# Seven half-size products for the layer-1 projections, K, Q, V and Z in single buffers on chip, and W_out written to DRAM as bf16

## The chip, the cores and the metric

The kernel runs on the 8 cores of one Trainium2 chip, each on one element of the batch; the cores exchange nothing. The metric is the device time of one execution on the slowest core, in microseconds (us).

## What is computed

Two layers, both `x <- LayerNorm(ALPHA * x + (mixer(x) * silu(z)) @ W_out)`, with S = D = 2048 per core. Layer 0 is the FoX mixer (16 heads of 128, forget gates), layer 1 is differential attention with 8 heads. Cut to layer 1, which the change touches most:

```python
def diff_mixer(h, w_in, lam_q, lam_k, subln_g, w_out, rel_bias, layer_idx):
    q, k, v, z = jnp.split(h @ w_in, [BRANCH, 2 * BRANCH, 3 * BRANCH], axis=-1)
    # q, k: (B, S, 8, 2, 128), two maps a head;  v: (B, S, 8, 256)
    for i in range(S // Q_BLOCK):            # 16 blocks of 128 rows, causal
        s = einsum('bqhmd,bkhmd->bhmqk', q[:, q0:kl], k[:, :kl]) * scale + bias
        p = softmax(where(mask, s, -inf))
        a = p[:, :, 0] - lam * p[:, :, 1]
        outs.append(einsum('bhqk,bkhe->bqhe', a.astype(v.dtype), v[:, :kl]))
    o = concatenate(outs, axis=1)
    o = o * rsqrt(mean(o * o, -1) + RMS_EPS) * subln_g * (1 - lambda_init)
    return (o * silu(z)) @ w_out
```

## The kernel before

Everything is bf16 in SBUF with f32 sums in PSUM. Two large buffers, A and B, of 65,536 bytes a partition each, hold transposed activations and then W_out; one more, M, is cut into small regions by offset (oW, oX, oS, oP, oT, oG). PSUM has eight banks `pb`.

**Order.** The code emits work items with a cost each into a planner. `Prog` derives waits from declared byte regions: an operation waits for every earlier one that wrote what it reads or used what it writes, and the region declared may be larger than the bytes touched. `Sched` carries a planner time `sc.t`; `sc.after(ns, fn)` emits `fn` once that time has gone by. `merge` and `merge_diff` weave two lists in proportion to their costs. Each engine then runs its own instructions strictly in emitted order, and so do the DMA queues: SP issues transposes, activations and outputs, POOL issues weights.

**Layer 0** projects its heads with `wino`: a 2x2 block product of half-size pieces is done as seven products instead of eight, with sums of weights and of x ahead (L401, VectorE) and sums of products behind (L546, L549, and the gate L539, VectorE). Products are 8 matmuls of 512 columns for Q and K (L498) or 32 of 128 columns for V and Z (L511). They write banks 0, 1 and 7, and the order of products is 1, 6, 7, 2, 5, 4, 3. Product 3 goes into the bank that 5 had.

**Epilogue 0** (`epi_block`, `epi_pair`): eight pairs of row blocks multiply the transposed gate (`gp0`, in B or M) by W_out (in A, loaded with a cast from f32 by the DMA of POOL's queue), 4 x 16 matmuls of 512 columns a block (`group`, L336), add the residual (L744), normalise, and write x1d (f32) and x1b (bf16, L796) to DRAM. `x1_tr` (L808) reads x1b back with a transposing DMA into B, column by column block.

**Layer 1** runs heads u = 0..7. `diff_qk` gives K and Q by plain products of 16 matmuls of 512 columns, `diff_vz` gives V and Z side by side, 16 matmuls of 512 columns for each of 16 row blocks, with a tanh, a gate (L914), a cast of V (L916) and the multiply by the norm's gain (L918), the last three on VectorE. K, Q, V and Z have two copies each, so the projections of head u run woven with the attention of head u-1. A block of attention is: scores (`mm_s`, L972), exp (L990 near the diagonal, L1014 away from it), row sums, a combination of both maps (`comb`, small operations L1031 to L1041, then L1043 over the whole row), a DMA transpose (L1048), the PV product (L1061, three accumulators in banks 5, 6, 7) and `diff_fin` (L1163 to L1184) into the gate. The maps live in a ring of 16,384 bytes, the transposed ones in another of 9,216.

**Epilogue 1** is as epilogue 0, with W_out in B and the gates in A, while the last head's attention drains.

The softmax here doesn't subtract the row's maximum and nothing guards it: scores larger than these inputs give would overflow.

## Time and profile before

| | us |
|---|---|
| median of 3 runs | 2792.17 |
| fastest and slowest run | 2779.47, 3180.02 |
| span of the profiled execution, slowest core | 2768.0 |
| spans of the eight cores | 2754.6 to 2768.0 |
| PE (TensorE) busy, share of the span | 2629.6, 95% |
| DVE (VectorE) busy | 1369.3, 49% |
| ACT (ScalarE) busy | 1240.4, 45% |
| POOL (GpSimd) busy | 214.4, 8% |

PE runs matmuls; PE's weight loads overlap them. A row of the waits names the engine that waited, its line, what it waited for, the sum, the number of times and the longest. A time is the device time of the whole execution, a span that of the profiled one from the first to the last instruction. The stages of the span: fox heads to about 1085 us, epilogue 0 to 1343 us, layer 1 from there, the heads' weave from 1456 us on, the last head and epilogue 1 from 2488 us.

### The profile page before, as it was taken

How to read it: one execution, taken by the hardware profiler on the slowest of the kernel's cores; microseconds unless marked ns; L12 is line 12 of the kernel's file. 1: busy time of each engine (PE TensorE's matmuls, PEld its weight loads, DVE VectorE, ACT ScalarE, POOL GpSimd, SP SyncE). 2: the span in 40 equal slices, each digit the busy share in tenths (PEclk: the TensorE clock that was granted, in tenths of full speed). 3: DMA queues.
4: the chain of work that ended last, by engine and by line, in shares of the span. 5: the costliest groups of instructions: out<-in, count | busy, mean ns of one | idle time of the engine just before them, and what ended most of it. 6: DMA issues, size and time to landing. Idle time of an engine off the chain costs nothing.

```text
span 2768.0 us, 60261 instructions; the slowest of 8 cores (2754.6 to 2768.0 us)
## 1 busy us (share of the span) xinstructions
PE 2629.6 (95%) x19886; PEld 1589.9 (57%) x20130; DVE 1369.3 (49%) x3834; ACT 1240.4 (45%) x3256; POOL 214.4 (8%) x412
## 2 busy tenths in 40 slices
PE   6799999999999998999999999999999999998998
PEld 4477777777777785444445544454545554543443
DVE  2544444444444443565423635455555455555666
ACT  0365555555555563343214443444444444533431
POOL 2000000000000000000000110111011111110110
PEclk9999999999999999999999999999999999999999
DMA  9222222223222239999814242534334344487653
GB/s 156 43 47 42 40 41 40 41 42 50 45 40 41 41 55 196 216 240 235 184 31 81 56 76 51 81 63 74 70 71 70 66 71 83 103 153 163 182 163 131
DMA packets 355728, 254.31 MB, mean 92 GB/s; under 512 B 280800, under 2 KB 298080, under 8 KB 350816
## 3 DMA queue, kind: packets, MB, share of 16 engines
q1 hardware_dynamic: 311184, 158.00, 24.3%
q0 software_dynamic: 44240, 92.44, 20.8%
q8 instruction: 168, 2.75, 0.4%
q14 instruction: 136, 1.11, 0.1%
HBM read 224.21 MB, written 58.26 MB: 102 GB/s over the span
## 4 chain that ended last, share of the span: by engine, by line
PE 84%; DMA 5%; DVE 3%; SPq 3%; issue 3%; ACT 1%; another core or an unknown queue 1%; DVEq 0%; POOL 0%; ACTq 0%; POOLq 0%
PE pb L336 42%; PE pb L511 13%; PE pb L498 13%; PE pb L655 4%; PE pb L640 4%; PE pb L1061 4%; PE pb L972 4%; DMA M<-M 2%; SPq L1210 1%; DMA x1b<-M 1%; DMA A<-xs 1%; DVE M L1043 1%; SPq L808 1%; ACT M L1014 1%
## 5 line engine op out<-in xcount | busy, mean ns | idle before, releaser
L643 ACT ACTIVATE M<-pb,M 128x256 bf16<-128x256 f32 (+1 forms) x1152 | 521.3, 461 | 408.5 <-PE pb L655 341.2
L336 PE MATMUL pb<-M,B 128*128 128x512 bf16 (+1 forms) x2122 | 526.2, 374 | 6.3 <-DVE M L916 3.7
L336 PE MATMUL pb<-B,M 128*128 128x512 bf16 x2058 | 517.5, 380 | 7.2 <-DMA B<-xs 3.8
L1014 ACT ACTIVATE M<-pb 128x512 bf16<-128x512 f32 (+3 forms) x512 | 264.6, 523 | 276.8 <-PE pb L972 249.1
L336 PEld LDWEIGHTS pb<-B,M 128*128 128x128 bf16 x2112 | 206.1, 98 | 204.4 <-issue 7.5
L655 PE MATMUL pb<-M 128*128 128x129 bf16 x2176 | 311.7, 221 | 1.8 <-DVE M L647 0.4
L640 PE MATMUL pb<-M 128*128 128x256 bf16 (+1 forms) x1152 | 307.0, 267 | 6.1 <-ACT M L643 4.6
L336 PEld LDWEIGHTS pb<-M,B 128*128 128x128 bf16 x2176 | 212.2, 98 | 174.7 <-issue 5.9
L655 PEld LDWEIGHTS pb<-M 128*128 128x128 bf16 x2176 | 206.5, 98 | 81.4 <-issue 5.4
L336 PE MATMUL pb<-B,A 128*128 128x512 bf16 x1002 | 236.2, 383 | 6.3 <-DMA B<-w1o 4.1
L511 PE MATMUL pb<-M,A 128*128 128x128 bf16 x3360 | 236.2, 219 | 0.1
L498 PE MATMUL pb<-A,M 128*128 128x512 bf16 x796 | 219.8, 383 | 15.2 <-DVE M L401 12.9
L511 PE MATMUL pb<-M,B 128*128 128x128 bf16 x3360 | 232.2, 219 | 2.2 <-DVE M L647 2.2
L1061 PE MATMUL pb<-M 128*128 128x256 bf16 x1088 | 210.8, 276 | 21.6 <-DMA M<-M 18.4
L972 PE MATMUL pb<-A 128*128 128x512 bf16 (+3 forms) x756 | 211.7, 319 | 17.5 <-ACT M L1014 9.3
L498 PE MATMUL pb<-B,M 128*128 128x512 bf16 x809 | 220.8, 379 | 1.5
L511 PEld LDWEIGHTS pb<-M,A 128*128 128x128 bf16 x3360 | 201.0, 98 | 3.6 <-issue 0.2
L511 PEld LDWEIGHTS pb<-M,B 128*128 128x128 bf16 x3360 | 199.4, 98 | 2.6 <-issue 2.3
L336 PE MATMUL pb<-A,B 128*128 128x512 bf16 x749 | 177.1, 384 | 15.1 <-DMA A<-w0o 14.0
L1061 PEld LDWEIGHTS pb<-M 128*128 128x128 bf16 x1088 | 105.7, 99 | 138.9 <-issue 27.6
L546 DVE TENSOR_TENSOR M<-pb,M 128x512 bf16<-128x512 f32 x150 | 103.5, 690 | 156.6 <-PE pb L640 124.8
L1043 DVE SCALAR_TENSOR_TENSOR M<-M 128x1152 bf16<-128x1152 bf16 (+15 forms) x128 | 173.0, 1352 | 5.6 <-DVE M L1041 0.4
(110 smaller groups left out, 2670.0 us busy)
## 6 DMA issues: line engine op xcount, KB each, us to landing
M<-w0s POOLq DMA_DIRECT2D x30, 1024.0 KB, 11.0
M<-x SPq DMA_DIRECT2D x16, 1024.0 KB, 6.2
x1d<-M SPq DMA_DIRECT2D x32, 512.0 KB, 5.2
M<-w1qk POOLq DMA_DIRECT2D x16, 1024.0 KB, 9.2
M<-w1vz POOLq DMA_DIRECT2D x8, 2048.0 KB, 17.2
M<-x1d SPq DMA_DIRECT2D x16, 1024.0 KB, 5.5
y<-M SPq DMA_DIRECT2D x32, 512.0 KB, 3.2
A<-w0o POOLq DMA_DIRECT2D x4, 2048.0 KB, 39.2
```

The costliest lines, as they stand in the source:

```text
L336: ins = e.matmul(out, lhsT=lhs(kc), rhs=rhs(kc), start=(kc == 0), stop=(kc == KC - 1))
L498: ins = e.matmul(pb[b][:, :], lhsT=w.ap[:, wo + kc * 128:wo + kc * 128 + 128], rhs=X.ap[:, xo + kc * 512:xo + kc * 512 + 512], start=(firs ...
L511: ins = e.matmul(pb[b][:, kk * 128:(kk + 1) * 128], lhsT=X.ap[:, xo + kc * 512 + kk * 128:xo + kc * 512 + kk * 128 + 128], rhs=w.ap[:, wo ...
L546: P.op("dve", lambda e: e.tensor_tensor(out=d, in0=shp(pb[b][:, :]), in1=shp(a.ap), op=ALU.add), reads=bank(b) + a.r, writes=rd)
L640: P.op("pe", lambda e: e.matmul(pb[s][:, 0:w], lhsT=F.k.ap[:, j * 128:(j + 1) * 128], rhs=F.q.ap[:, i0 * 128:i0 * 128 + w], start=True, st ...
L643: P.op("act", lambda e: e.activation(out=pt.ap[:, 0:w], in_=pb[s][:, 0:w], func=AF.Exp, bias=bs.ap[:, j * 8 + I:j * 8 + I + 1], scale=SCAL ...
L655: P.op("pe", lambda e, n=n, k=k, first=first: e.matmul(pb[b][:, k * 129:(k + 1) * 129], lhsT=pt.ap[:, n * 128:(n + 1) * 128], rhs=F.v3[:, ...
L808: P.dma("sp", "xt", lambda e: e.dma_start_transpose(out=d, in_=x1b[b * 128:(b + 1) * 128, :]), reads=[("x1b", b, b + 1)], writes=rx("B", t ...
L972: P.op("pe", lambda e: e.matmul(pb[s][:, o:o + nb * 128], lhsT=Dv.q3[:, m, i * 128:(i + 1) * 128], rhs=Dv.k3[:, m, j0 * 128:(j0 + nb) * 12 ...
L1014: P.op("act", lambda e: e.activation(out=self.p.ap[:, lo:lo + nb * 128], in_=pb[s][:, 0:nb * 128], func=AF.Exp, scale=SCALE, accum_out=st. ...
L1043: P.op("dve", lambda e: e.scalar_tensor_tensor(out=self.p.ap[:, 0:w], in0=self.p.ap[:, w:2 * w], scalar=c(15), in1=self.p.ap[:, 0:w], op0= ...
L1061: o = P.op("pe", lambda e, j=j: e.matmul(pb[b][:, 0:256], lhsT=self.t.ap[:, j * 128:(j + 1) * 128], rhs=Dv.v3[:, j, :], start=(j == 0), st ...
```

## The change

- Layer 1 projects by `unit1`: for each of K, Q, V, Z and each half p of the rows one unit of seven products with the class `Wino`, which layer 0 uses too. Weights come as four quarters per unit pair (`load_w1`) and get four sums of 1024 columns (`sum_w`) on VectorE. The sums of x for layer 1 take the first 49,152 bytes of A.
- With A taken, K and Q stand once in A, V and Z once in M. Projection banks are 0, 1, 7; PV accumulators 5 and 6. Head 0's K and Q, p=0, stay plain (`plain1`).
- The order of a head becomes: V and Z of head u with its upper blocks' attention, then K and Q of head u+1, p=1 and then p=0, with the lower blocks'. Where a buffer would be overwritten, `DT.clear` or a drain empties the attention first.
- The gate of Z is a multiply in place on VectorE (L961); the gain multiply is on POOL (L962). One constant of `comb` moves to POOL too; its row sums are one operation (L1095) for both maps.
- The maps, and their transposes, share one ring of 23,072 bytes with first fit. The transposed map takes the place of the second map.
- W_out of both layers is cast by DRAM-to-DRAM DMAs (`cast_wo`, 32 of them, during fox heads 1 to 8 and diff heads 1 to 4) and then loaded as bf16.
- In epilogue 0 `gp0[6]` moves from M to chunk 7 of B, and `gp0[7]` within M. Epilogue 1's buffers move.

```diff
+        def sum_w(w, base=0):
+            at = lambda k: ((k - base) % 7) * 1024
+            for out, a, b in ((4, 1, 0), (1, 3, 1), (5, 3, 4), (6, 2, 5)):
+                sl = lambda k: w.ap[:, at(k):at(k) + 1024]
+                rl = lambda k: w.rr(at(k), at(k) + 1024)
...
+        xp1 = [[V("B", p * 32768 + k * 8192, 8192) for k in range(4)] + [V("A", p * 24576 + k * 8192, 8192) for k in range(3)] for p in range(2)]
+        XSUMS = ((4, 2, 3, ALU.add), (5, 4, 0, ALU.subtract), (6, 1, 5, ALU.subtract), (2, 0, 2, ALU.subtract))
...
+                def done(k, b):
...
+                    elif k == 6:
+                        tt(T, T, b)
+                    elif k == 7:
+                        tt(U, T, b)
...
+                            copy(11, b)
+                    elif k == 5:
+                        add(22, U, b)
+                    elif k == 4:
+                        add(21, T, b)
+                    else:
+                        add(12, T, b)
+                return sum([product(k, b, f) for k, b, f in ((1, x, True), (6, y, True), (7, h, True), (2, x, False), (5, y, True), (4, h, False), (3, y, False))], [])
...
-        gp0 = [V("B", c * 8192, 8192) for c in (7, 6, 5, 4, 7, 6)] + [V("M", oS[1] + c * 8192, 8192) for c in range(2)]
+        gp0 = [V("B", c * 8192, 8192) for c in (7, 6, 5, 4, 7, 6, 7)] + [V("M", oS[1], 8192)]
...
+        wot = [[V("A", p4 * 16384, 16384) for p4 in range(4)],
+               [V("B", p4 * 16384, 16384) for p4 in range(4)]]
+        def cast_wo(li, n):
+            p4, c = n // 4, n % 4 * 2
+            P.dma("pool", "cw%d" % (n % 4), lambda e: e.dma_start(out=wob[li][p4, c:c + 2], in_=wo_in[li][p4, c:c + 2]), writes=[("wob%d" % li, n, n + 1)])
...
+        def load_wo(li, p4, h=None):
+            w = wot[li][p4]
+            lo, hi = (0, 8) if h is None else (4 * h, 4 * h + 4)
+            P.dma("pool", "wo%d_%d" % (p4, lo), lambda e: e.dma_start(out=runs(w.ap)[:, lo:hi, :], in_=wob[li][p4, lo:hi].rearrange("c p e -> p c e")),
...
+            if b >= 12:
+                sc.after(3500, lambda: x_late.append(b - 12))
...
-                s = u % 2
-                b = s * 24576
...
-                self.q = V("A", b, 8192)
-                self.k = V("A", b + 8192, 8192)
-                self.z = V("A", b + 16384, 8192)
-                self.v = V("M", oS[0] + s * 8192, 8192)
+                self.q = V("A", 49152, 8192)
+                self.k = V("A", 57344, 8192)
+                self.v = V("M", oS[0], 8192)
+                self.z = V("M", oS[0] + 8192, 8192)
...
+        w1 = [V("M", o_, WSL) for o_ in oW1]
...
+        def load_w1(u, t):
+            w = w1[t % 2]
+            P.dma("pool", "w1s%d" % (t % 2), lambda e: e.dma_start(out=runs(w.ap[:, 3072:7168]), in_=w1s[u, t].rearrange("c p e -> p c e")), writes=w.rr(3072, 7168))
...
+            def dst(c):
+                m, st = int(c % 10 == 2), 2 * p + (c > 20)
+                made(t, p, u)
+                if t in (K_, Q_):
+                    d, lo = (Dv.k, Dv.q)[t], m * 2048 + st * 512
+                    return d.ap[:, lo:lo + 512], d.rr(lo, lo + 512)
...
+            def gate(src, rsrc, H, c):
+                if H is None:
+                    return t == Z_
+                d, rd = dst(c)
+                m = int(c % 10 == 2)
+                gn = gain.ap[:, m * 128:m * 128 + 128].unsqueeze(1).to_broadcast([128, 4, 128])
+                P.op("dve", lambda e: e.scalar_tensor_tensor(out=H.ap, in0=H.ap, scalar=1.0, in1=src, op0=ALU.add, op1=ALU.mult), reads=rsrc + H.r, writes=H.r)
+                P.op("pool", lambda e: e.tensor_tensor(out=d, in0=b4(H.ap), in1=gn, op=ALU.mult), reads=H.r + gain.r, writes=rd)
+            return W1.unit(w1[t % 2], xp1[p], t in (K_, Q_), dst, gate)
...
-                P.op("dve", lambda e: e.scalar_tensor_tensor(out=zt.ap, in0=t.ap, scalar=1.0, in1=z, op0=ALU.add, op1=ALU.mult),
-                     reads=bank(b) + t.r, writes=zt.r)
-                P.op("dve", lambda e: e.tensor_copy(out=Dv.v3[:, blk, :], in_=pb[b][:, 0:256]),
-                     reads=bank(b), writes=Dv.v.rr(blk * 256, blk * 256 + 256))
-                P.op("dve", lambda e: e.tensor_tensor(out=Dv.z3[:, blk, :], in0=zt.ap, in1=gain.ap, op=ALU.mult),
-                     reads=zt.r + gain.r, writes=Dv.z.rr(blk * 256, blk * 256 + 256))
...
-                self.p = rP.get(w * 4)
+                self.p = [rP.get(w * 2), rP.get(w * 2)]
...
-                if not rA.fits(w * 2):
-                    sc.after(500, self.comb)
-                    return
...
-                        P.op("dve", lambda e, m=m: e.reduce_sum(out=c(10 + m), in_=c(m * 5, k), axis=AX.X), reads=rc(m * 5, k), writes=rc(10 + m))
...
-                    P.op("dve", lambda e: e.tensor_tensor(out=c(12, 2).unsqueeze(2), in0=c(10, 2).unsqueeze(2), in1=s3, op=ALU.add),
...
+                    s3 = st.ap[:, 0:10].rearrange("p (m c) -> p m c", m=2)[:, :, 0:k + 1]
+                    P.op("dve", lambda e: e.reduce_sum(out=c(10, 2).unsqueeze(2), in_=s3, axis=AX.X), reads=rc(0, k + 1) + rc(5, k + 1), writes=rc(10, 2))
...
-                P.op("dve", lambda e: e.scalar_tensor_tensor(out=self.p.ap[:, 0:w], in0=self.p.ap[:, w:2 * w], scalar=c(15), in1=self.p.ap[:, 0:w],
-                                                             op0=ALU.mult, op1=ALU.add),
...
+                P.op("dve", lambda e: e.scalar_tensor_tensor(out=self.p[0].ap, in0=self.p[1].ap, scalar=c(15), in1=self.p[0].ap, op0=ALU.mult, op1=ALU.add),
+                     reads=self.p[0].r + self.p[1].r + rc(15), writes=self.p[0].r)
+                P.op("pool", lambda e: e.tensor_scalar(out=c(16), in0=c(a), scalar1=c(a), scalar2=256.0 * RMS_EPS, op0=ALU.mult, op1=ALU.mult), reads=rc(a), writes=rc(16))
+                self.t = self.p[1]
...
-                    self.acc = 5 + self.no % 3
+                    self.acc = 5 + self.no % 2
...
-                free = lambda b: cnt["acc"] < 3 and b.ready is not None and (b.i % 2 or cnt["gb"] < 2)
+                free = lambda b: (cnt["acc"] < 2 and b.ready is not None and (b.i % 2 or cnt["gb"] < 2)
+                                  and own.get((V_, 0)) == b.u and (b.i < 8 or own.get((V_, 1)) == b.u) and own.get((Z_, b.i // 8)) == b.u)
...
+        def merge_diff(F, share=1.0, tail=0.0, burst=700.0, drain=True):
+            left = sum(c for c, _ in F) - tail
+            owed = DT.owed() * share
...
-                while ct < cost and cf >= lead + (tf - lead) * ct / (cost or 1):
+                while credit > 0 and owed > 0:
                     x = DT.next()
                     if x is None:
+                        credit = min(credit, burst)
...
-                    ct += x[0]
+                    credit -= x[0]
+                    owed -= x[0]
...
+                credit += it[0] * owed / max(left, it[0], 1.0)
+                left -= it[0]
                 sc.run(it)
...
+                if 1 <= u <= 8:
+                    F.insert(len(F) // 4, call(cast_wo, 0, 2 * u - 2))
+                    F.insert(3 * len(F) // 4, call(cast_wo, 0, 2 * u - 1))
...
+        pj["banks"] = [0, 1, 7]
+        for t in (K_, Q_):
+            F = plain1(0, t)
+            for n in range(len(F), 0, -4):
+                F.insert(n, call(late_sums))
+            sc.merge(F, [])
+            sum_w(w1[t], 4)
...
+        F = unit1(0, K_, 1) + [call(load_w1, 0, V_), (0.0, lambda: sc.after(13000, lambda: sum_w(w1[0], 4)))]
+        for n, f in enumerate(sum_x(xp1[0])):
+            F.insert(2 + n * 2, (0.0, f))
         sc.merge(F, [])
...
+        def nxt(u, t):
+            load_w1(u, t)
+            sc.after(14000, lambda: sum_w(w1[t % 2], 4))
+        for u in range(ND - 1):
+            F = unit1(u, V_, 1) + [call(DT.clear, u - 1)] + unit1(u, V_, 0) + [call(nxt, u + 1, K_)]
+            F += unit1(u, Z_, 1) + unit1(u, Z_, 0) + [call(nxt, u + 1, Q_)]
+            if 1 <= u < 5:
+                for n in range(4):
+                    F.insert((2 * n + 1) * len(F) // 8, call(cast_wo, 1, 4 * u - 4 + n))
+            DT.add(u, HI)
+            merge_diff(F, 0.75)
+            diff_E(u + 1)
+            DT.add(u, LO)
+            merge_diff(unit1(u + 1, K_, 1) + unit1(u + 1, Q_, 1), 0.6)
+            F = unit1(u + 1, K_, 0) + [call(nxt, u + 1, V_)] + unit1(u + 1, Q_, 0) + [call(nxt, u + 1, Z_)]
+            merge_diff(F, tail=5000)
...
+        u = ND - 1
+        DT.clear(u - 1)
+        F = unit1(u, V_, 0) + unit1(u, Z_, 0) + [call(load_wo, 1, p4) for p4 in range(2)] + [call(load_gp, p4, 0, 14) for p4 in range(3)]
+        F += unit1(u, V_, 1) + unit1(u, Z_, 1) + [call(load_wo, 1, 2), call(load_wo, 1, 3), call(load_rows, 1)]
+        DT.add(u, range(12))
+        merge_diff(F, 0.9)
```

PE, end of epilogue 0; A is W_out, B and M hold gates (`gp0`), `dq_sp_xt` are the x1 transposes and `dq_sp_gz7_0` is the load of `gp0[7]`. Before:

```order
L336 MATMUL pb<-A,M 128x512 [waits ms_dve]
L336 MATMUL pb<-A,M 128x512 x15
L336 MATMUL pb<-A,M 128x512 [waits ms_dve]
L336 MATMUL pb<-A,M 128x512 x15
L336 MATMUL pb<-A,M 128x512 [waits dq_sp_gz7_0,ms_dve]
L336 MATMUL pb<-A,M 128x512 x15
```

After:

```order
L337 MATMUL pb<-A,B 128x512 [waits ms_dve]
L337 MATMUL pb<-A,B 128x512 x13
L337 MATMUL pb<-A,B 128x512 [waits dq_sp_xt]
L337 MATMUL pb<-A,B 128x512
L337 MATMUL pb<-A,M 128x512 [waits dq_sp_gz7_0,ms_dve]
L337 MATMUL pb<-A,M 128x512 x15
```

The last two matmuls of block 13, ahead of blocks 14 and 15, now stand behind a transpose of x1.

PE, start of layer 1, where the last strip of x1 is first needed (`dq_sp_xt`). Before, after three plain strips of K and Q:

```order
L336 MATMUL pb<-B,M 128x512 [waits ms_act]
L336 MATMUL pb<-B,M 128x512 x15
L336 MATMUL pb<-B,M 128x512 [waits dq_sp_xt,ms_dve]
L336 MATMUL pb<-B,M 128x512 x15
L336 MATMUL pb<-B,M 128x512 [waits ms_dve]
L336 MATMUL pb<-B,M 128x512 x15
```

After, behind two plain strips:

```order
L337 MATMUL pb<-B,M 128x512 [waits ms_act]
L337 MATMUL pb<-B,M 128x512 x15
L514 MATMUL pb<-B,M 128x512 [waits ms_dve]
L514 MATMUL pb<-B,M 128x512 x7
L514 MATMUL pb<-A,M 128x512 [waits ms_act]
L514 MATMUL pb<-A,M 128x512 x7
```

Products of 8 matmuls, which read sums of x from A, take the place of groups of 16.

DVE, in the V,Z part of a head. Before, the gate, cast and gain operations of a row block between those of attention:

```order
L1038 RECIPROCAL M<-M 128x1
L1039 SCALAR_TENSOR_TENSOR M<-M 128x1
L1041 SCALAR_TENSOR_TENSOR M<-M 128x1
L1043 SCALAR_TENSOR_TENSOR M<-M 128x1280
L914 SCALAR_TENSOR_TENSOR M<-M,pb 128x256
L916 CAST M<-pb 128x256
L918 TENSOR_TENSOR A<-M 128x256
```

After, with L559 a product sum, L1067 the near maps, L1254 the PV output and L1102 the comb:

```order
L961 SCALAR_TENSOR_TENSOR M<-M 128x512
L559 TENSOR_TENSOR M<-pb,M 128x512
L1067 SCALAR_TENSOR_TENSOR M<-M 128x256 x2
L1254 SCALAR_TENSOR_TENSOR M<-pb,M 128x256
L559 TENSOR_TENSOR M<-pb,M 128x512
L961 SCALAR_TENSOR_TENSOR M<-M,pb 128x512
L1095 TENSOR_REDUCE M<-M 128x2
L1099 RECIPROCAL M<-M 128x1
L1100 SCALAR_TENSOR_TENSOR M<-M 128x1
L1102 SCALAR_TENSOR_TENSOR M<-M 128x1536
```

Sums of 512 columns now stand between the near maps and the combs, in the one order of DVE.

## Rows read from the trace of the kernel before

**Rows 1.** Cores: span and mean granted clock of TensorE

```profile
core 0: 2768.0 us, clock 0.987
```

**Rows 2.** First part of the page: busy time, share and instructions by engine

```profile
PE 2629.6 (95%) x19886; PEld 1589.9 (57%) x20130; DVE 1369.3 (49%) x3834; ACT 1240.4 (45%) x3256; POOL 214.4 (8%) x412
```

**Rows 3.** Windows: length, busy (x) PE, PEld, DVE, ACT, POOL, clock, DMA share, GB/s

```profile
97.00:1010.00 913.00, 905.33 (x10701) 707.16 (x10771) 428.52 (x1048) 532.63 (x1158) 20.76 (x28) 1.00 0.24 41
1070.00:1210.00 140.00, 121.66 (x723) 63.02 (x732) 64.52 (x161) 48.38 (x121) 7.01 (x14) 0.95 0.96 222
...
1455.70:1595.40 139.70, 138.91 (x727) 72.09 (x741) 72.22 (x240) 64.19 (x198) 16.11 (x31) 1.00 0.38 69
1595.40:1753.70 158.30, 146.29 (x737) 73.13 (x750) 75.23 (x247) 64.13 (x203) 17.95 (x35) 0.98 0.34 62
...
2184.60:2329.90 145.30, 141.95 (x733) 72.66 (x746) 73.89 (x244) 64.23 (x202) 17.76 (x35) 0.99 0.39 69
...
2487.70:2768.00 280.30, 250.19 (x1189) 118.18 (x1211) 175.46 (x443) 87.43 (x271) 27.57 (x54) 0.96 0.60 162
```

**Rows 4.** Waits of PE, 1455.7 to 2329.9 us: line, releaser, sum, times, longest

```profile
PE pb L972 <- ACT M L1014: 7.3, 14, 2.6
PE pb L972 <- ACT M L990: 4.6, 8, 0.7
```

**Rows 5.** Timeline of PE: start, us, engine, line, count, idle before

```profile
1344.29 55.41 PE L336 MATMUL pb<-B,M 128*128 128x512 bf16 x250 [0.96 <-DVE M L744]
1399.54 2.75 PE L336 MATMUL pb<-M,B 128*128 128x512 bf16 x12
```

**Rows 6.** Chain in order of time: start, us, what

```profile
1069.12 9.09 PE pb L511 x160
```

**Rows 7.** Timeline of PE, epilogue 0, the waits on W_out

```profile
1092.43 1.86 PE L336 MATMUL pb<-A,B 128*128 128x512 bf16 x4 [6.87 <-DMA A<-w0o]
...
1112.40 2.72 PE L336 MATMUL pb<-A,B 128*128 128x512 bf16 x6 [7.10 <-DMA A<-w0o]
```

**Rows 8.** Windows behind those waits

```profile
1092.40:1097.00 4.60, 4.57 (x15) 1.91 (x16) 0.78 (x3) 1.08 (x3) 0.00 (x0) 0.61 1.04 271
1112.40:1116.00 3.60, 3.38 (x10) 1.53 (x12) 0.00 (x0) 0.57 (x2) 0.00 (x0) 0.50 1.14 253
```

**Rows 9.** DMA issues: queue, count, KB each, us from issue to landing

```profile
A<-w0o POOLq DMA_DIRECT2D x4, 2048.0 KB, 39.2
...
B<-x1b SPq DMA_TRANSPOSE x16, 7.3
```

**Rows 10.** Timeline of SP's queue, the transposes of x1 blocks 12 and 15

```profile
1323.05 8.93 SPq L808 DMA_TRANSPOSE B<-x1b  x1
...
1364.32 6.92 SPq L808 DMA_TRANSPOSE B<-x1b  x1
```

**Rows 11.** Groups by form: busy, mean ns, idle before and what ended it

```profile
L336 PE MATMUL pb<-B,A 128*128 128x512 bf16 x1002 | 236.2, 383 | 6.3 <-DMA B<-w1o 4.1 <-DVE M L744 1.0
...
L546 DVE TENSOR_TENSOR M<-pb,M 128x512 bf16<-128x512 f32 x150 | 103.5, 690 | 156.6 <-PE pb L640 124.8 <-PE pb L498 21.3 <-PE pb L655 6.1
...
L401 DVE TENSOR_TENSOR M<-M 128x1024 bf16<-128x1024 bf16 x120 | 77.4, 686 | 4.0 <-DVE M L401 0.9 <-issue 0.2
...
L916 DVE CAST M<-pb 128x256 bf16<-128x256 f32 x128 | 53.4, 417 | 0.0
...
L539 DVE SCALAR_TENSOR_TENSOR M<-M 128x512 bf16<-128x512 f32 x30 | 20.7, 688 | 13.3 <-ACT M L535 13.3
...
L1043 DVE SCALAR_TENSOR_TENSOR M<-M 128x2048 bf16<-128x2048 bf16 x8 | 18.8, 2352 | 0.3
L1033 DVE TENSOR_TENSOR M<-M 128x2 f32<-128x2 f32 x112 | 18.1, 162 | 12.4 <-DVE M L1031 0.9
```

**Rows 12.** One line's instructions: duration in ns, least, median, longest

```profile
L1164 POOL TENSOR_TENSOR M<-M x128: 182/195/2192, 1489.8 to 2681.8; 128x1 f32<-128x1 f32 x128
...
L1165 POOL TENSOR_TENSOR M<-M x128: 549/551/2311, 1490.1 to 2682.2; 128x1 f32<-128x1 f32 x128
```

458 lines of the change are left out of this document (213 added, 245 removed).

## The prediction, made before the changed kernel had run

> **What bounds the kernel now.** I read the spans first: the slowest core takes 2768.0 us at a granted clock of 0.987 [rows 1]. The shortest of the three runs is 11.5 us above that span and the median 24.2 us, so I add 18 us to a span to get a time. The page's first part puts TensorE (PE) at 95% [rows 2]. The windows by stage say where the other 5% is: while the fox heads run (97 to 1010 us) PE is busy 905.3 of 913.0 us; a diff head takes 139.7 to 158.3 us and PE is busy at least 92% of each; the end of layer 1 has 30 us idle out of 280 [rows 3]. Inside the six middle heads the named waits of PE are small: 7.3 us for the last exponentials and 4.6 for the near ones, in six heads together [rows 4]. So the bound is the stream of matmuls itself, and a change pays if it makes that stream shorter without new waits.
>
> Two rows give the price of the stream. 256 matmuls of 512 columns run from 1344.29 to 1399.54, which is 0.2158 us each [rows 5]; 160 matmuls of 128 columns take 9.09 us, 0.0568 each [rows 6]. Half-size products over 128 columns cost 5% more per column than over 512 (4 x 0.0568 = 0.227), which the V,Z part has to pay.
>
> **(a) K and Q.** Before, a head has 256 matmuls of 512 columns for K and Q; seven products of 8, in 4 units, are 224. That is 32 fewer for seven heads and 16 fewer for the first (its p=0 stays plain): 240 x 0.2158 = **-51.8 us**.
>
> **(b) V and Z.** Before 256 x 0.2158 = 55.2 us a head; after 4 units x 7 x 32 = 896 x 0.0568 = 50.9. Eight heads: **-34.8 us**.
>
> **(c) W_out of layer 0 read as bf16.** PE waits 6.87 and 7.10 us for it [rows 7], and runs at a granted clock of 0.61 and 0.50 behind these waits [rows 8], near the lower of its two levels, for 8.2 us of work, of which about 3.6 us are lost. The load is 4 DMAs of 2 MB at 39.2 us each [rows 9]; the bf16 copy halves what is read. The next thing that is late there are the transposed gates, which share the same DMA window at a share of 0.96 [rows 3]. Between 6 and 18 us come back; I take **-14**. The 32 casts from DRAM to DRAM run beside fox heads and diff heads with DMA shares of 0.24 and 0.34 to 0.39 [rows 3] and cost nothing; with no cover, what waits would be W_out itself, as now.
>
> **(d) A new wait at the end of epilogue 0.** The gate of blocks 12 and 13 (gp0[6]) moves from M to chunk 7 of B. The order shows, two matmuls before the end of block 13, a wait on the transposes of x1 that was not there: the transpose of block 12 writes into the same declared region. Blocks 14 and 15 (128 matmuls, 27.6 us) end at 1343.33, 0.96 us before the first K,Q matmul at 1344.29 [rows 5], so block 13 ends at 1315.7. The transpose of block 12 is issued at 1323.05 [rows 10] and lands 7.3 us later [rows 9], at 1330.4. PE stands 1330.4 - 1315.7 = 14.7 us, with blocks 14 and 15 queued behind it, and some 2 us more of lower clock after the pause: **+17** (12 to 19). Behind it everything of x1 for blocks 14 and 15 is late by the same amount, so the next stage does not win it back.
>
> **(e) Start of layer 1.** Only the plain p=0 halves of K and Q, 128 matmuls or 27.6 us, now stand between the last block and the first matmul that needs the last strip; before, 192 (41.4 us). The last transpose is issued at 1364.32 [rows 10], lands at 1371.6, and 1344.29 + 27.6 = 1371.9: just covered. But the seven-product operands come after it: four sums of the late block on VectorE, 4 x 0.69 = 2.8 us, and the 16 sums of the first half, 11 us, fed between matmuls (688 ns each from L401's form [rows 11]). I take **+5** (2 to 12).
>
> **(f) Waits inside the heads.** A middle head takes 145.7 us on average ((2329.9 - 1455.7)/6) [rows 3], of which the shortest one, 139.7 us with PE idle for 0.8, is nearly pure stream. Without new waits heads go to about 145.7 - 6.9 - 4.3 = 134.5. VectorE (DVE) now works 72 to 75 us in a head [rows 3]. Off: 8 casts of 512 columns for K and Q at the 0.69 of such a sum, 16 x 3 operations of 256 columns for V and Z at the 0.417 of L916, and two small ones of about 0.16 (as L1033) in each of 16 blocks: -5.5 - 20.0 - 5.1. On: 40 product sums at 0.690, 8 gates at 0.688, 16 weight sums at 0.686: +27.6 + 5.5 + 11.0 [rows 11]. Sum 74 + 13.5, about 88 us, 65% of a head, and more in the V,Z part. In the fox heads the same scheme runs with DVE at 428.5 of 913 us (47%), and PE idle for under 1% [rows 3]. What is tight: product 3 goes into the bank of product 5 and waits for its DVE sum, with one product of 1.7 to 1.8 us (32 x 0.0568, 8 x 0.2158) ahead. The sum takes 0.69 us; a comb (L1043) in front of it holds DVE up to 2.35 us [rows 11], which leaves 2.35 + 0.69 - 1.75 = 1.3 us of stall. With 8 units in a head and a long comb in front of one in four, that is 2.6 us; add something for one accumulator less (two for three) and for single K, Q, V, Z buffers, whose forced drains cost where attention is not fed evenly: **+3 us a head, +21 over seven** (0 to 15 a head).
>
> **(g)** Epilogue 1 gets a bf16 W_out too; its wait for it was 4.1 us [rows 11], and two of the four loads come later than the others, so I count 0 (4 either way).
>
> **Sum:** -51.8 - 34.8 - 14 + 17 + 5 + 21 = **-57.6**; span 2768.0 - 57.6 = 2710, time 2710 + 18 = **2728 us**.
>
> **The POOL multiply.** The gain of Z moves to POOL: 8 multiplies of 512 per head. No row has one. From below the nearest row is POOL's own one-column multiply, L1164, 0.2 us; from above its worst, 2.2 us, since L1164 and L1165 stretch from medians of 0.195 and 0.551 us to 2.19 and 2.31 [rows 12]: about a comb's length, so POOL is held while DVE runs one. At 2.3 us each, 8 are 18 us of POOL a head, beside 18 us that it has [rows 3]: POOL stays under 30% and nobody but the PV fin of the next half head needs Z. I take 0 on the path.
> The Trainium skill (GPSIMD Engine Reference, section 3.1, Elementwise) gives about 2.6 cycles an element, an estimate of 1.1 us for 512; and SBUF — State Buffer, "Who interferes with whom", says that a DVE operation with two SBUF inputs contends with a GpSimd operation that reads SBUF, and that the first to start blocks the other. The trace agrees in one direction (L1165 up to 2.31 us); by that rule the multiply would also hold DVE, 8 x 1.1 = 9 us a head, 62 us in seven if all of it came to lie on the path, which gives about 2790.
>
> **The rivals.**
> - *The saving whole* (0.20): the fox heads show that DVE at 47% is no hindrance, and if 65% isn't either, f is 0; the loads give -18 and the transition +2: 2768 - 86.6 - 18 + 17 + 2 = 2682, time **2700**. Against it: every unit has the tight sum above.
> - *DVE and POOL in each other's way* (0.25): DVE at 65 to 70%, in the V,Z part more, long combs and POOL multiplies between its operations. If 6 to 8 us more than before stand in each head instead of 3, with up to 12 in some, f is 42 to 63: time **2749 to 2770**. Eight POOL multiplies that hold DVE for 1 us each, between the 0.2 and 2.3 of POOL's rows, give 8 x 7 = 56 and 2763; For it: the stretched L1165. Against: DVE idles over a third of the time. This is the case into which the Trainium skill's rule on the shared ports (SBUF — State Buffer, "Who interferes with whom") falls.
> - *Slower* (0.05): the sum of product 5 comes late in each unit by the longest comb, 2.35 us, in all 8 units of a head: 18.8 x 7 = 132 in place of 21, time **2839**. From (2792 - 2707)/7 = 12 us a head on the kernel is no faster (2707 being the time with f at 0). Against: only one comb in sixteen is that long [rows 11].
> - *The wait (d) is not there, or W_out's waits remain* (0.05): blocks 12 and 13 may drift so that the transpose is down in time: 2728 - 17 = 2711; or gates take the place of W_out as the late ones: 2728 + 14 = 2742. It moves the others rather than replaces them.
> - The forecast itself, **2712 to 2745**, has 0.45.
>
> **How the numbers follow.** 8 in 10 reach from a little below the whole saving (2690) to the contention case's upper part (2775). This kernel's measurement can tell about 2% from no change, and 2% below 2792 is 2736. Below that lie the whole saving (0.20), over half of the forecast (0.29) and the shifted case (0.04), with a little of the others: 0.55. Slower needs over 2848: 0.03. The rest is 0.42.
>
> **What would show it.** (a, b) PE's instruction count and the matmul groups' busy time fall; the span from the first to the last V,Z stage tells the head: 137 us right, 134 the whole saving, over 141 contention. (c) No waits on W_out behind 1090 us. (d) One wait of 12 to 17 us of PE for a transpose from x1b near the end of epilogue 0. (e) A wait on DVE sums of 2 to 10 us behind the plain K,Q. (f) Waits of PE on the lines of the product sums (L556, L559), of 1 to 2 us, many of them; POOL's multiply (L962) between 0.2 and 2.3 us. Wrong would be: heads of more than 146 us, or PE waits inside them on attention's exponentials or transposes in place of the sums.

## The result and the profile after

The changed kernel takes **2827.5 us** (median of 4 runs, 2824.9 to 2908.3) against 2785.8 for the kernel before beside it: a ratio of **1.0163**, 95% interval 1.0129 to 1.0198. The prediction was 2728 us, with a range of 2690 to 2775. Forecast and result differ in sign. Every ratio here leaves out the executions in which the cores of one die ran at a lower granted clock: one of the four of each kernel (2908.3 us here), and all six of y_share below, which has no ratio for that reason.

The cores and the first part of the page of the kernel after, which answer to [rows 1, 2]:

```profile
core 6: 2824.9 us, clock 0.968
...
PE 2575.8 (91%) x25010; PEld 1785.2 (63%) x25010; DVE 1524.6 (54%) x3572; ACT 1253.0 (44%) x3240; POOL 346.7 (12%) x644
```

PE's busy time fell by 54 us, and the span grew by 57: PE now stands still 249 us where it was 138. The ratio means 45 us. The span of the kernel before is 11.5 us under the shortest of its times, where in the other profiles 1.5 to 1.6 us lie between the two, so some 10 of the 57 us are of that one trace. To see where, the span is cut at three matmuls that both kernels have: the first of epilogue 0, the first of layer 1, and the first of epilogue 1. Windows of the kernel before, and of the one after (columns as in [rows 3]):

```profile
1078.48:1344.29 265.81, 239.39 (x1177) 113.66 (x1200) 140.97 (x345) 100.37 (x248) 15.29 (x32) 0.96 0.94 232
1344.29:2486.14 1141.85, 1106.79 (x5655) 560.72 (x5770) 560.04 (x1833) 470.87 (x1468) 132.00 (x261) 0.99 0.43 77
2486.14:2768.00 281.86, 251.75 (x1197) 118.92 (x1218) 176.31 (x445) 88.30 (x273) 28.45 (x55) 0.96 0.60 161
```

```profile
1084.26:1363.79 279.53, 239.00 (x1205) 113.31 (x1203) 140.20 (x343) 99.24 (x248) 15.28 (x32) 0.93 0.84 209
1363.79:2531.14 1167.35, 1052.53 (x10709) 759.78 (x10708) 733.38 (x1654) 503.85 (x1519) 250.91 (x475) 0.97 0.45 80
2531.14:2824.90 293.76, 245.99 (x1163) 114.33 (x1160) 159.20 (x366) 68.96 (x206) 32.87 (x57) 0.92 0.54 164
```

Epilogue 0 is 13.7 us longer, layer 1 is 25.5 longer, epilogue 1 is 11.9 longer; 5.8 us stand ahead of epilogue 0. These are the slowest cores. By the medians of the eight cores the four differences are 6.5 us ahead of epilogue 0, 6.9 in it, 20.4 in layer 1 and 13.5 in epilogue 1. Those ahead of epilogue 0 are no chance of the core: before, it starts at 1076 to 1082 us on the eight cores, after at 1084 to 1087, and in b_cast below, which has the same casts beside the fox heads, at 1077 to 1086. What they are wasn't tested. In layer 1 PE's busy time did shrink, by 54 us although six more blocks of the last head's attention are now done in it, but its idle time grew from 35 to 115 us.

Waits of PE in the six middle heads of the kernel after (1455 to 2328 us; line, releaser, sum, times, longest), the answer to [rows 4]:

```profile
PE pb L1038 <- ACT M L1080: 24.5, 11, 4.8
PE pb L1120 <- DVE M L1254: 24.4, 18, 3.0
PE pb L1038 <- ACT M L1056: 20.7, 18, 2.7
...
PE pb L527 <- DVE M L556: 0.2, 1, 0.2
```

L1038 are the scores, L1080 and L1056 the far and near exponentials, L1120 is PV, L1254 what empties its accumulator. The only wait on a product sum is the last row, 0.2 us. And the middle heads take as long as before, with a lower clock. Windows of the six together, and then of the rest of layer 1, each for the kernel before and for the one after:

```profile
1455.70:2329.90 874.20, 849.82 (x4381) 434.58 (x4468) 443.43 (x1458) 385.06 (x1204) 104.20 (x206) 0.99 0.38 68
1455.00:2328.00 873.00, 798.53 (x8121) 577.99 (x8119) 548.41 (x1243) 394.85 (x1194) 195.02 (x376) 0.97 0.45 79
...
2329.90:2486.14 156.24, 146.14 (x770) 75.52 (x784) 88.83 (x311) 71.95 (x234) 23.90 (x50) 0.99 0.68 129
2328.00:2531.14 203.14, 169.10 (x1858) 129.56 (x1856) 120.08 (x296) 79.88 (x247) 51.91 (x91) 0.94 0.48 88
```

PE is busy 133.1 us in a middle head where it was 141.6, and idle 12.4 where it was 4.1. Behind the six heads it is idle 34.0 us where it was 10.1; one wait for a far exponential there is 10.7 us long.

The timeline of PE in epilogue 0 of the kernel after shows the two waits there (idle before the row in brackets); none on W_out is left, the answer to [rows 7]:

```profile
1287.10 29.12 PE L337 MATMUL pb<-A,B 128*128 128x512 bf16 x126 [22.66 <-DMA B<-gtd]
...
1333.07 1.01 PE L337 MATMUL pb<-A,B 128*128 128x512 bf16 x2 [16.85 <-DMA B<-x1b]
```

The second was forecast, at 14.7; on the other seven cores it is 10.1 to 14.7 us. The first was 6.4 us before. It is 13.3 to 14.5 us on six of the eight cores and 22.7 and 24.6 on two; before, 4.9 to 7.4.

### The profile page after: what moved, and what is told of

Read it like the earlier page. It is cut to its first block, busy times and chain, and to the rows that moved or that the text cites. A ratio compares the mean times of both kernels' runs of the same rounds, so it can differ in the third digit from the quotient of the medians.

```text
span 2824.9 us, 70454 instructions; the slowest of 8 cores (2800.4 to 2824.9 us)
## 1 busy us (share of the span) xinstructions
PE 2575.8 (91%) x25010; PEld 1785.2 (63%) x25010; DVE 1524.6 (54%) x3572; ACT 1253.0 (44%) x3240; POOL 346.7 (12%) x644
## 4 chain that ended last, share of the span: by engine, by line
PE 75%; DMA 8%; DVE 6%; issue 4%; SPq 4%; ACT 1%; POOL 1%; DVEq 0%; another core or an unknown queue 0%; ACTq 0%; POOLq 0%
PE pb L514 25%; PE pb L527 23%; PE pb L337 13%; PE pb L688 4%; PE pb L673 4%; PE pb L1120 3%; PE pb L1038 3%; DMA M<-M 2%; DMA x1b<-M 2%; SPq L860 1%; SPq L1282 1%; DMA A<-xs 1%; DMA B<-wob 1%; DVE M L1102 1%; SPq L741 1%
## 5 line engine op out<-in xcount | busy, mean ns | idle before, releaser
L527 PE MATMUL pb<-M,B 128*128 128x128 bf16 x7456 | 539.1, 222 | 0.2 <-DVE M L556 0.2
L514 PE MATMUL pb<-B,M 128*128 128x512 bf16 x1800 | 478.1, 383 | 1.7 <-DVE M L559 1.3
L527 PE MATMUL pb<-M,A 128*128 128x128 bf16 x6432 | 452.2, 219 | 13.3 <-issue 8.4
L514 PE MATMUL pb<-A,M 128*128 128x512 bf16 x1560 | 415.8, 382 | 16.6 <-DVE M L399 12.9
L527 PEld LDWEIGHTS pb<-M,A 128*128 128x128 bf16 x6432 | 392.8, 98 | 33.0 <-issue 15.4
L559 DVE TENSOR_TENSOR M<-pb,M 128x512 f32<-128x512 f32 x322 | 221.9, 689 | 241.2 <-PE pb L527 116.1
L1080 ACT ACTIVATE M<-pb 128x512 bf16<-128x512 f32 (+3 forms) x512 | 264.9, 522 | 180.2 <-PE pb L1038 137.2
L1038 PE MATMUL pb<-A 128*128 128x256 bf16 (+3 forms) x768 | 217.8, 323 | 68.2 <-ACT M L1080 40.3
L337 PE MATMUL pb<-B,A 128*128 128x512 bf16 x1024 | 231.6, 383 | 21.1 <-DMA B<-wob 21.1
L1120 PE MATMUL pb<-M 128*128 128x256 bf16 x1088 | 203.2, 277 | 46.2 <-DVE M L1254 34.3
L556 DVE TENSOR_TENSOR M<-pb,M 128x512 bf16<-128x512 f32 x198 | 135.8, 689 | 201.4 <-PE pb L673 126.9
L337 PE MATMUL pb<-A,B 128*128 128x512 bf16 x896 | 205.8, 382 | 39.5 <-DMA B<-gtd 22.7
L514 PEld LDWEIGHTS pb<-A,M 128*128 128x128 bf16 x1560 | 143.5, 99 | 115.0 <-issue 23.5
L337 PEld LDWEIGHTS pb<-B,A 128*128 128x128 bf16 x1024 | 101.0, 99 | 137.2 <-issue 24.8
L1102 DVE SCALAR_TENSOR_TENSOR M<-M 128x1920 bf16<-128x1920 bf16 (+15 forms) x128 | 173.0, 1352 | 14.8 <-DVE M L1100 0.7
L1120 PEld LDWEIGHTS pb<-M 128*128 128x128 bf16 x1088 | 98.8, 99 | 116.7 <-issue 60.3
## 6 DMA issues: line engine op xcount, KB each, us to landing
wob<-w0o POOLq DMA_DIRECT2D x16, 512.0 KB, 13.8
```

The costliest lines, as they stand in the source:

```text
L337: ins = e.matmul(out, lhsT=lhs(kc), rhs=rhs(kc), start=(kc == 0), stop=(kc == KC - 1))
L514: ins = e.matmul(pb[b][:, :], lhsT=w.ap[:, wo + kc * 128:wo + kc * 128 + 128], rhs=xs.ap[:, kc * 512:kc * 512 + 512], start=(first and kc ...
L527: ins = e.matmul(pb[b][:, kk * 128:(kk + 1) * 128], lhsT=xs.ap[:, kc * 512 + kk * 128:kc * 512 + kk * 128 + 128], rhs=w.ap[:, wo + kc * 12 ...
L556: P.op("dve", lambda e: e.tensor_tensor(out=d, in0=shp(pb[b][:, :]), in1=shp(a.ap), op=ALU.add), reads=bank(b) + a.r, writes=rd)
L559: P.op("dve", lambda e: e.tensor_tensor(out=o.ap, in0=pb[b][:, :], in1=a.ap, op=ALU.add), reads=bank(b) + a.r, writes=o.r)
L1038: P.op("pe", lambda e: e.matmul(pb[s][:, o:o + nb * 128], lhsT=Dv.q3[:, m, i * 128:(i + 1) * 128], rhs=Dv.k3[:, m, j0 * 128:(j0 + nb) * 12 ...
```

## The experiments

My theory after the trace had four parts: the waits in the heads come from the map ring, from the casts beside the heads, and from the forced drains with their two accumulators; the wait (d) in epilogue 0 is a false one; the late gate is an order in SP's queue; and epilogue 1 waits for W_out by its own order. Rivals: the POOL multiply; and that W_out as bf16 gains nothing.

All ratios are to the kernel before, run beside each on the same chip. Each carries its 95% interval. The chips differ between experiments, so two kernels are compared by their ratios, and 0.001 of ratio is 2.8 us. The ratios of b_cast, y_base, x_castfox and f_dvegain rest on two executions each.

### W_out as bf16 alone

The edit adds the 32 casts and the bf16 load to the kernel before, at the places in the fox heads and diff heads where the change has them.

> The kernel before, with one part of the change: W_out of both layers cast to bf16 in DRAM by 32 DMAs and loaded from there. My theory (the gain moves on to the next thing that is late): the two waits on W_out in epilogue 0 (14.0 us) go, and the wait for the transposed gate of blocks 12 and 13 grows from 6.4 us to about 20 us, because SP issues that transpose in the same place; layer 1 starts within 5 us of 1344, and the whole is 0 to 8 us faster than before. Rival (c of the prediction): the gain stays, 14 us faster.

Measured: **0.9943** (0.9924 to 0.9963). The theory fell. Epilogue 0 takes 248.9 us against 265.8 on the slowest cores, so -16.9 against the -14 of the prediction, and -13.8 by the medians of the eight cores (262.5 and 248.7). The gate wait is 5.5 us there and 7.8 to 11.0 on the other seven cores: it grows by some 3 us, not to 20. Waits of PE in the six middle heads of b_cast:

```profile
PE pb L1066 <- DMA M<-M: 12.8, 6, 4.2
```

Those are PV waits on map transposes, 2.1 us in the kernel before. This is the worst of the eight cores: the others have 3.4 to 8.1 us, and 0.4 to 1.1 before. Layer 1 takes 1152 us for 1142 on the slowest cores; the medians are 1141.3 and 1140.4. The next run moves the casts that run beside the diff heads:

```diff
+                if 9 <= u <= 14:
+                    for n in range(3 * (u - 9), min(16, 3 * (u - 9) + 3)):
+                        F.insert((2 * (n % 3) + 1) * len(F) // 6, call(cast_wo, 1, n))
```

> As b_cast, but the 16 casts of layer 1's W_out run beside fox heads 9 to 14 and not beside diff heads 1 to 4. In b_cast layer 1 took 1152 us up to epilogue 1 against 1142 in the kernel before, with 12.8 us of PE waits on map transposes in six heads against 2.1. Theory: these 10 us are the casts in the way of the map transposes; they come back, and the whole is 22 to 28 us faster than before (ratio about 0.991). Rival: the 10 us are a shift of attention's order; layer 1 stays at 1150.

Measured: **0.9923** (0.9894 to 0.9952), about 21 us. Window of b_cast2 from the first V,Z load (1341.0 us) to epilogue 1 (2471.2):

```profile
1341.00:2471.20 1130.20, 1107.24 (x5733) 556.79 (x5732) 554.29 (x1821) 467.68 (x1464) 130.37 (x259) 0.99 0.40 76
```

Between the same two marks b_cast takes 1143.8 us (1342.6 to 2486.4) and the kernel before 1133.6. So on the slowest cores the casts beside the diff heads cost 13.6 us. By the medians of the eight cores layer 1 goes from 1141.3 to 1135.5, 5.8 us, and that is also what the timed ratios give: a step of 0.002, within the intervals. The waits on map transposes are down to 0.5 to 3.7 us. The casts do cost something there, nearer 6 us than 14.

### Two accumulators alone

```diff
-                    self.acc = 5 + self.no % 3
+                    self.acc = 5 + self.no % 2
...
-                free = lambda b: cnt["acc"] < 3 and b.ready is not None and (b.i % 2 or cnt["gb"] < 2)
+                free = lambda b: cnt["acc"] < 2 and b.ready is not None and (b.i % 2 or cnt["gb"] < 2)
```

> The kernel before, with one part of the change: two PV accumulators in place of three. My theory (short accumulators are one of three causes of the new waits inside the heads, about 4.5 us a head with the half clock behind them): PE's waits of PV on the line that empties the accumulator appear, 2 to 4 us a head, and the time rises by 20 to 40 us. Rival: the accumulators only bind when attention is drained in a lump, as the changed kernel does it; in the kernel before, where it is fed evenly, nothing changes (under 8 us).

Measured: **1.0003** (0.9992 to 1.0014). The rival holds: with attention fed evenly two accumulators do. The accumulator wait is 2.1 us in three times over the whole span. The time hides a shift, though: by the medians layer 1 is 8 us longer and epilogue 1 6 us shorter than in the kernel before.

### The false wait in epilogue 0

```diff
-                                    lambda k0, k1, t=t: t.rr(k0 * 256, k1 * 256)))
+                                    lambda k0, k1, t=t, lo=lo: sum([t.rr(k * 256 + lo, k * 256 + lo + 128) for k in range(k0, k1)], [])))
```

> The changed kernel, with the reads of the transposed gate in epilogue 0 declared by the columns that a block really reads, so that the last two matmuls of block 13 no longer wait for the transpose of x1 block 12. Theory: the wait of 16.9 us goes and 15 to 20 us of the time with it. Rival: the transposes of x1 for blocks 12 to 15 are late for another reason, and the wait moves to the start of layer 1; under 5 us faster.

Measured: **1.0094** (1.0078 to 1.0109), 19 us below the changed kernel. The wait is gone: block 13 reads other columns than the transpose of block 12 writes. The kernels whose names begin with x, y, z and f build on this one.

```diff
-                F.insert(12, (0.0, lambda: sc.after(8000, lambda: (load_gp0(6, 0, 16), load_gp0(7, 0, 16)))))
+                F.insert(2, (0.0, lambda: load_gp0(6, 0, 16)))
+                F.insert(12, (0.0, lambda: sc.after(8000, lambda: load_gp0(7, 0, 16))))
```

> As a_exact, and the transposing load of the gate of blocks 12 and 13 is emitted one x1 transpose and one residual load earlier in SP's queue. Theory (the wait of 22.7 us for that gate is SP's order, not the bandwidth): the load is issued some 14 us earlier and 10 to 16 us more come back than in a_exact. Rival: the transposing DMAs are limited by traffic, and the wait stays above 15 us.

Measured: **1.0087** (1.0067 to 1.0108), no step from a_exact. Another 10 to 16 us had been expected. The wait fell from 14.5 to 5.0 us on the slowest core, and on six of the eight it is gone; yet a new wait of 3.2 us stands in the plain K,Q of layer 1, on the line that empties their bank (L978). VectorE is late with it, since a sum of x ahead of it waits 3.4 us for a transpose of x1. SP's order did set the gate's wait, and taking it away doesn't move what comes next. It was tried again at the end, on the fastest version of then:

> z_share with the transposing load of the gate of blocks 12 and 13 emitted earlier, as in a_early. There PE's wait for it fell from 14.5 to 5.0 us, and the time didn't move. Theory: what follows (the last x1 transposes and their sums) ends by SP's queue, not by PE, so again within 4 us of z_share. Rival: 7 to 10 us faster.

Measured: **0.9855** (0.982 to 0.9889), z_share beside it 0.9838. No gain, as expected.

### POOL or VectorE for the gain multiply

```diff
-                P.op("pool", lambda e: e.tensor_tensor(out=d, in0=b4(H.ap), in1=gn, op=ALU.mult), reads=H.r + gain.r, writes=rd)
+                P.op("dve", lambda e: e.tensor_tensor(out=d, in0=b4(H.ap), in1=gn, op=ALU.mult), reads=H.r + gain.r, writes=rd)
```

> a_exact with the gain multiply of Z on VectorE again, 8 a head, in place of POOL. Rival of the prediction (the POOL multiply and VectorE block each other): each head gets 4 to 9 us shorter, 30 to 60 us in all. My theory now (POOL holds nobody up; the waits come from the map ring, the tanh in ACT's queue and the accumulators): no gain, and up to 10 us slower by 8 x 0.69 us more on VectorE in a head.

Measured: **1.0135** (1.0119 to 1.0151), 11 us slower than a_exact; layer 1 is 1174 us by the medians for 1160. The same edit on z_e1 (below), where no larger wait covers it:

> z_e1 with the gain multiply on VectorE. With the lumps gone it is the clean test of the rival on POOL. If POOL's multiply (1.27 us each, 8 a head) holds VectorE up, this is faster by up to 8 x 7 x 1 = 56 us. My theory: POOL holds nobody on the path; between 0 and 15 us slower than z_e1, ratio 0.975 to 0.980.

Measured: **0.9867** (0.9803 to 0.9932) against 0.9747 of z_e1: slower by 1.2%, 33 us, where at most 15 were expected; by the medians the spans are 23 us longer. So in neither kernel does the multiply on POOL cost the time that the rival gave it. One line's instructions in the kernel after, the multiply on POOL:

```profile
L962 POOL TENSOR_TENSOR M<-M x64: 1255/1273/1291, 1472.1 to 2537.4; 128x512 bf16<-128x512 f32 x64
```

But the rival's mechanism is real, and small. Two lines of VectorE that read both their inputs from SBUF, in a_exact and then in x_dvegain (shortest, median and longest in ns):

```profile
L1067 DVE SCALAR_TENSOR_TENSOR M<-M x256: 274/418/2178, 1407.0 to 2615.5; 128x256 bf16<-128x256 f32 x120, 128x128 bf16<-128x128 f32 x8
L1100 DVE SCALAR_TENSOR_TENSOR M<-M x128: 218/219/1272, 1412.7 to 2624.1; 128x1 f32<-128x1 f32 x128
...
L1067 DVE SCALAR_TENSOR_TENSOR M<-M x256: 277/419/427, 1397.0 to 2615.9; 128x256 bf16<-128x256 f32 x120, 128x128 bf16<-128x128 f32 x8
L1100 DVE SCALAR_TENSOR_TENSOR M<-M x128: 219/219/221, 1402.7 to 2624.5; 128x1 f32<-128x1 f32 x128
```

Without the multiply on POOL the long ones are gone. In the kernel after 36 instructions of VectorE are stretched, each of them beside a multiply on POOL, by 22.5 us in all, 2.8 us a head; product sums that read PSUM (L559) take 0.691 us with or without it. On VectorE the eight multiplies take 8 x 0.692 = 5.5 us a head, more than that.

### Three accumulators, two score banks

```diff
-            s = 2 + cnt["s"] % 3
+            s = 2 + cnt["s"] % 2
...
-                    self.acc = 5 + self.no % 2
+                    self.acc = 4 + self.no % 3
...
-                free = lambda b: (cnt["acc"] < 2 and b.ready is not None and (b.i % 2 or cnt["gb"] < 2)
+                free = lambda b: (cnt["acc"] < 3 and b.ready is not None and (b.i % 2 or cnt["gb"] < 2)
```

> a_exact with three PV accumulators (banks 4 to 6) and two score banks (2 and 3) in place of two and three. Theory: the waits of PV on the emptying of an accumulator (24 us in six heads) go, with the half clock behind the one of 3.0 us; but the scores wait for the exponentials more often, so that it ends between 15 us faster and 15 us slower. It tells which of the two banks is scarcer: if the score waits grow by less than 24 us in six heads, accumulators were.

Measured: **1.0091** (1.0075 to 1.0107), as a_exact. The accumulator waits (24.4 us in six heads) are gone, and the score waits went from 24.1 and 20.7 to 36.0 and 27.0 us. The score waits grew by 18.2 us, less than the 24.4 that went, so by the rule set ahead of the run the accumulators were the scarcer ones; but the time doesn't move. Two scarce banks change places.

### The map ring

The slot of the first map goes back to the planner 5 us after the comb is emitted. The edit makes it 9:

```diff
-                sc.after(5000 + w, lambda: rP.live.remove(self.p[0]))
+                sc.after(9000 + w, lambda: rP.live.remove(self.p[0]))
```

> a_exact with a slot of the map ring given free 4 us later in the planner's time, so that the next map isn't written where a transpose still reads. Theory: ACT's wait on a map transpose (23.3 us, 7 times in six heads) goes, PE's wait behind it (3.6 us a head, 4.6 with the near one) falls to under 1 us, and with the half clock behind it 4 to 6 us a head come back: 25 to 40 us. Rival: the ring is simply too small at that point; the planner then holds scores back and has to drain them in a lump at the end of the stage, where the waits reappear; within 10 us of a_exact.

Measured: **0.9980** (0.9969 to 0.9990), 31 us below a_exact. One thing that it does is seen on ACT. Waits of ACT in the six middle heads, in the kernel after and in x_ring (core 1):

```profile
ACT M L1080 <- DMA M<-M: 23.3, 7, 4.7
```

```profile
ACT M L1080 <- DMA M<-M: 10.8, 5, 3.4
```

An exponential may not write a slot that a transpose still reads. It stands at the head of ACT's queue until the transpose has landed, and the scores of the next blocks stand behind it, PE with them. This wait was to go and only halves, and it isn't the whole gain. PE's waits on the far exponentials in these heads fall from 24.5 to 15.3 us, those on an accumulator from 24.4 to 17.9, and those on the near exponentials rise from 20.7 to 25.9. By the medians of cores 0 to 3 against a_exact, 18 of the gained us lie in the six middle heads, 9 ahead of head 0's first gate and 5 behind the middle heads. A later release shifts the whole weave of scores and projections, and the runs don't part the wait for the transpose from that shift. Then the casts are moved as in b_cast2, once without the ring's edit and once with it:

> a_exact with only the casts of layer 1's W_out moved beside fox heads 9 to 14 (the ring's slots are given free as early as in the changed kernel). It separates the two causes that y_base takes away together. If the early release alone makes exponentials wait for a transpose that still reads, the wait of 3.6 us a head stays and the gain is under 10 us (ratio to before 1.006 or more). If it takes a transpose that the casts made late, the waits go in all heads and the ratio is as y_base's, 0.993 to 0.998.

Measured: **1.0098** (1.0074 to 1.0123); ACT still waits 20.9 us in six times. The casts alone were not the cause.

> x_ring with the casts of layer 1's W_out beside fox heads 9 to 14, not beside diff heads. Theory: casts make the map transposes land late, and a late transpose is what keeps the map ring busy, so the remaining waits of ACT on a map transpose (11.1 us in six heads in x_ring) go, and heads 1 to 4 get 1 to 2 us shorter each: 8 to 15 us faster than x_ring (ratio to before 0.998), so about 0.994. Rival: with the later release the ring no longer depends on the casts; within 4 us of x_ring.

Measured: **0.9933** (0.9911 to 0.9954), and no wait of ACT on a map transpose is left. Heads on its core 5 take 139.6 us each. So the two causes hang together. As I read it, with the early release a transpose is in the way in any case, with the later one only those that the casts make late. One head of y_base in four windows (the Z units; K,Q p=1 and K p=0; Q p=0; the V units), and under it the same four of the kernel after:

```profile
1557.41:1599.93 42.52, 38.23 (x538) 33.78 (x536) 29.69 (x57) 20.00 (x61) 17.87 (x21) 1.00 0.36 59
1599.93:1651.92 51.99, 49.04 (x263) 25.75 (x262) 34.61 (x98) 20.54 (x65) 12.61 (x28) 0.97 0.36 68
1651.92:1665.64 13.72, 13.72 (x89) 7.50 (x88) 6.09 (x11) 3.88 (x12) 4.01 (x10) 1.00 0.53 97
1665.64:1697.01 31.37, 30.54 (x471) 27.40 (x469) 21.45 (x46) 20.52 (x63) 1.59 (x6) 1.00 0.53 86
```

```profile
1601.01:1647.99 46.98, 39.16 (x528) 35.33 (x526) 27.20 (x51) 19.00 (x54) 14.97 (x20) 0.93 0.49 82
1647.99:1702.29 54.30, 50.59 (x272) 26.60 (x271) 34.73 (x99) 22.41 (x72) 11.08 (x31) 0.97 0.33 60
1702.29:1715.98 13.69, 13.69 (x89) 7.51 (x87) 6.09 (x11) 3.99 (x12) 4.04 (x10) 1.00 0.55 97
1715.98:1747.23 31.25, 30.41 (x471) 27.40 (x470) 23.26 (x49) 20.36 (x63) 2.93 (x9) 1.00 0.78 120
```

The 6.6 us between the sums lie in the first two windows. In the first the clock is 1.00 for 0.93: PE's pause of 3.6 us had cost its own length and a stretch at the lower level behind it.

> y_base with slots given free another 4 us later (13 in place of 9 us). Theory: 9 us covered most, so at most 5 us faster; if the ring is now too small, waits come back as drains and it is 5 to 20 us slower. It brackets the best time of release.

Measured: **0.9955** (0.9940 to 0.9971): slower, if anything. The accumulator waits doubled (17.8 to 34.3 us). By the medians layer 1 is 34 us longer and epilogue 1, with less attention left for it, 20 us shorter. So between 9 and 13 us the release no longer pays in the heads; values between weren't tried.

### The forced drain

```diff
-            merge_diff(unit1(u + 1, K_, 1) + unit1(u + 1, Q_, 1), 0.6)
+            merge_diff(unit1(u + 1, K_, 1) + unit1(u + 1, Q_, 1), 0.8)
```

> y_base with 0.8 in place of 0.6 of the owed attention woven into the K,Q p=1 units, so that less is left for the forced drain behind them. Theory: the wait of 3.0 us on an accumulator in each head belongs to that forced drain and goes, with the half clock behind it: 3 to 5 us a head, 20 to 35 us. Rival: attention then runs short in the units of p=0, or the drain only moves; within 8 us.

It has no ratio. In its trace, on cores 4 to 7, a head takes 136.5 us for 139.6. The same kernel again:

> y_share again, timed: in its profile the four cores of the second die show heads of 136.5 us against 139.6 in y_base, and the accumulator wait of 3.0 us a head gone. Theory: 3 us a head in seven heads, about 22 us under y_base, ratio to before 0.984 to 0.988. Rival: the next stage pays it back; 0.993.

Measured: **0.9838** (0.9815 to 0.9860), 26 us below y_base; by the medians 19 of them lie in the heads, and most of the rest ahead of epilogue 0, which y_base, on another chip, starts 7 us later. Waits of PE in the middle heads of y_base (core 7) and of z_share:

```profile
PE pb L1120 <- DVE M L1254: 17.8, 6, 3.1
```

```profile
PE pb L1120 <- DVE M L1254: 1.3, 6, 0.3
```

K of the next head overwrites the one buffer of K, so all scores of the lower blocks must be out first; what was not woven in ran in a lump. That its short PV groups used two accumulators faster than VectorE empties them is my reading; what is shown is that the wait goes when the lump gets smaller.

### The tanh ahead of the exponentials

The edit emits the tanh of Z's gate 0.9 us after the sum that it reads, in place of directly behind it. In it, a gate can read a sum that the next part has overwritten, so only its order counts.

> y_base with the tanh of Z's gate emitted 0.9 us later in the planner's time, so that ACT does not stand at it, with exponentials behind it, while VectorE still makes the sum. Theory: PE's waits on the near exponentials (25 us in six heads) fall by 10 us or more, 5 to 15 us faster than y_base. Rival: these waits are the plain length of one exponential between two score groups; nothing changes.

Measured: **0.9939** (0.9919 to 0.9958), as y_base. The near waits fell from 25.9 to 7.9 us, and the accumulator waits rose from 17.8 to 29.4. With 0.5 and 0.6 us, on z_e1:

> z_e1 with the tanh of Z's gate emitted 0.5 us later and its multiply 0.6 us after that (1.1 us in all, as long as before). In y_tanh, with 0.9 and 0.7, the waits on the near exponentials fell from 25.9 to 7.9 us in six heads, but those on an accumulator rose from 17.8 to 29.4. Theory: with the drain woven in (z_share) the accumulators have room, so the gain stays: 10 to 20 us faster than z_e1, ratio to before 0.968 to 0.971. Rival: the waits only change place again; 0.974 to 0.976.

Measured: **0.9765** (0.9716 to 0.9813) against 0.9747. The near waits are 16.8 us for 31.1 in the whole span, and the time doesn't move; why it doesn't stays open.

### Epilogue 1

```diff
+            if n == 0 and li:
+                order = [(pa, 0), (pa, 1), (pb_, 0), (pb_, 1), (pa, 2), (pb_, 2), (pa, 3), (pb_, 3)]
...
-            merge_diff(F, 1.0 / max(1, 4 - n))
+            merge_diff(F, (0.6, 0.6, 0.8)[n] if n < 3 else 1.0)
```

> z_share with epilogue 1 rearranged: its first two blocks multiply the first two quarters of W_out before either needs the third, and more of the last head's attention is woven into the first blocks. Theory: PE's wait of 17 to 21 us on the third quarter, which can be loaded only after the last projection, falls to under 8 us and 8 to 15 us come back. Rival: the queues of SP and POOL then hold up the transposes of the gate; no gain.

Measured: **0.9747** (0.9728 to 0.9766), 2702 us: 25 us below z_share and 70 below the kernel before. The two edits were not parted, and the gain is larger than the 8 to 15 us expected; all of it lies in epilogue 1 (290.5 to 262.7 us by the medians). The wait on W_out (21.7 us in z_share) does not show any more; a wait of 9.2 us for the residual addition that empties a bank (L789) is new. Its page:

```profile
PE 2554.3 (95%) x25010; PEld 1770.5 (66%) x25010; DVE 1525.2 (56%) x3572; ACT 1246.3 (46%) x3240; POOL 379.6 (14%) x644
```

This version beats both kernels. It has all of the change, and six edits of order and declaration on it.

## Why the prediction was wrong, by its own steps

- **What bounds the kernel.** Right as a reading, wrong as a rule for what comes next. PE's stream did bind; once it is shorter, waits that were small or hidden before are what binds.
- **(a), (b)** Right, and seen where the new waits are mostly gone: in five heads of z_share, at a granted clock of 1.00, PE is busy 130.1 us a head. The 141.6 of before less the 11.2 forecast are 130.4. Layer 1 was forecast at 1141.8 - 86.6 + 21 + 5 = 1081 us, 1094 with the attention moved into it (see g); z_share takes 1096 by the median.
- **(c)** -14 forecast, -13.8 by the medians in b_cast and -16.9 on the slowest cores. Right. In the changed kernel the wait for the gate of blocks 12 and 13 grew from between 4.9 and 7.4 us to between 13.3 and 24.6. "The transposed gates" were named as the next late thing and priced at nothing. The faster W_out alone doesn't do that (5.5 to 11.0 us in b_cast); the order of SP's queue does (a_early), and what makes that queue later in the changed kernel stays open. Nor does the wait have a price of its own, since without it the time stays. With (d) taken away epilogue 0 is 9.3 us shorter than before by the medians, 13.7 in z_e1. That the casts cost nothing was wrong in the diff heads, by about 6 us (b_cast2), 14 on the slowest cores.
- **(d)** Right, mechanism and size: 16.85 us for 14.7 on the slowest core, 10.1 to 14.7 on the others, and 19 us with what follows for 17. It was read from the order alone.
- **(e)** The waits there sum to 5.3 us (2.7, 2.2 and 0.4) for 5. Right. 4.9 of them are waits on product sums (L556, L559) that stand between the sums of x in VectorE's order.
- **(f)** This is the step that failed. The price was put on the sum behind product 5: 3 us a head. There PE waits 0.2 us in six heads; VectorE worked 91 us a head, close to the 88 forecast, and no product sum held PE up. The wait was in the attention: (24.5 + 24.4 + 20.7)/6 = 11.6 us a head. PE's idle time is 12.4 us a head where 4.1 + 3 were forecast, and its busy time 133.1 where the shorter stream would be 130.4, 2.7 more at a lower granted clock (0.97). So a head took 145.5 us where 137.5 was forecast, 48 us in the six middle heads. The prediction's own sign of being wrong, waits on attention's exponentials in place of the sums, is what came. "Single K, Q, V, Z buffers, whose forced drains cost" stood in the step as a thing to be added and had no number; and the one map ring, which the section on the change names, was in no step. The later release of its slots is the largest single gain, 31 us, against 26 for the smaller drain.
- **(g)** Forecast 0. Epilogue 1 is 11.9 us longer although 57 of 136 tile columns of the last head's attention have left it, some 13 us by the prices of [rows 5, 6]. So it was wrong by 25 us: the two late loads of W_out make a wait of 21.1 us. The prediction had seen them and took the wait of before, 4.1 us, as the size.
- **The POOL multiply.** 0 on the path was assumed. Each takes 1.273 us, inside the bounds of 0.2 and 2.3, and together they stretch VectorE's instructions by 2.8 us a head. What of that reaches the path isn't known; moving the multiplies to VectorE costs more.
- **The rivals.** "DVE and POOL in each other's way" names a mechanism that the trace shows, at a fraction of its price; as the cause of the slowdown it is out by two runs. The slower rival had nearly the right size (2839) and the wrong place, which is luck. Its point of decision, 12 us a head, was nearly reached by another mechanism (11 us over the 134.5 of a head without new waits). Its chance of 0.05 counted only one way in which a head can lose 12 us.
- By stage, against a span of 2710: epilogue 0 and what is ahead of it +16.5, layer 1 +86, epilogue 1 +12, together 115. Of the 86, 13 are the attention that came over from epilogue 1 and 48 stand in the six middle heads; the other 25 weren't taken apart, but PE's idle time behind these heads (34.0 us for 10.1) is where most of them must be. In times the miss is 99.5 us, 2827.5 for 2728: the trace of before has a span well under the times of that kernel, which the 18 us added to it made up for.

## What to carry to other kernels

When a change turns double buffers into single ones to pay for a shorter stream, price the lumps and not the averages: list what must be empty before each buffer is written again, and see how long the queue, the ring and the banks take for what is then done in one go. A ring whose slots are given back by a planned time is a wait of its own: compare that time with when the reader's DMA really lands. A wait of some microseconds that stands just behind the one you remove needs a price too: ask what sets it, and what stands behind it in turn. Here the gate's wait grew, and taking it away gained nothing, since the next thing was as late. And a false dependency can be seen in the order of instructions before anything has run.

## What the runs showed of the hardware that was not expected

- POOL multiplies 512 f32 elements a partition, with bf16 out, in 1.273 us, and nearly the same each time (1.255 to 1.291). Beside it VectorE gives way: instructions with both inputs in SBUF are stretched, L399 (a sum of weights) from 0.683 to 1.255 us, L1067 from 0.418 to as much as 2.183, L1100 from 0.219 to as much as 1.267. With the multiply on VectorE (x_dvegain) the longest of these are 0.694, 0.427 and 0.221 us. The Trainium skill's page GPSIMD Engine Reference, section 3.1, with 2.6 cycles an element, gave an estimate of 1.1 us; the measurement decides. L1235, one column wide, ran up to 2.48 us in the same kernel, against a median of 0.551. There POOL gives way: beside each of its 18 long ones VectorE was already running such an instruction, a comb in the longest.
- 16 DMAs of 512 KB from DRAM to DRAM made PE wait 3.4 to 12.8 us for map transposes in six heads of the kernel before, against 0.5 to 3.7 without them (b_cast and b_cast2, eight cores each), at a DMA share of about 0.4 in the heads. Beside the fox heads of the kernel after 16 of them raise the DMA share from 0.24 to 0.30, and PE is busy 903.8 of 913.0 us as against 905.3.
- A pause of PE of 3.6 us is paid again in part: the granted clock in the 47 us around it is 0.93, and 1.00 in the same part of a head without it (y_base). In six heads with such pauses PE's busy time is 2.7 us a head over that of the stream at full clock.
